# Gate projection of a branch merge made in two earlier stages and kept in DRAM

## What is computed

```python
h = rms_norm(x, g_mix_pre)
(lru_x, lru_gate, pool_in, q, k, v, q_idx, k_idx, w_idx,
 gate_logits) = split_columns(h @ w_in, IN_SIZES)
ya = rg_lru(conv(lru_x), ...) * gelu(lru_gate)        # recurrence
yb = multiscale_pool(pool_in, w_pool, pool_scale)
yc = dsa_attention(q, k, v, q_idx, k_idx, w_idx)      # index masks, attention
up = einsum('bsnc,ncd->bsnd', stack([ya, yb, yc], axis=2), w_branch)
gates = sigmoid(gate_logits.reshape(b, s, 3, 1024) + b_gate)
merged = sum(gates * up, axis=2)
```

## Time and profile before

| | us |
|---|---|
| median of 3 runs | 4222.14 (4216.18 to 4222.91) |
| the profiled execution, its own time | 4222.38 |
| its span, first to last instruction | 4220.3 |
| recurrence | 58.4 |
| index masks | 105.1 |
| attention and turn | 110.7 |
| merge | 225.4 |

### The profile page before, as it was taken

The page is one execution under the profiler, slowest core; times in us unless marked ns, Lnnn a source line. Parts: engine busy times, 40 slices in busy tenths (PEclk is TensorE's granted clock), DMA queues, the critical chain, the costliest instruction groups (busy, mean ns, idle before and its releaser), DMA issues. The chain is left out here.

```text
span 4220.3 us, 45269 instructions
## 1 busy us (share of the span) xinstructions
PE 3577.3 (85%) x17433; PEld 2585.9 (61%) x17433; DVE 2311.1 (55%) x2911; ACT 1676.4 (40%) x2523; POOL 1518.4 (36%) x748
## 2 busy tenths in 40 slices
PE   5999979967969999965996999995925999568997
PEld 3778869954446666652664555554813666447876
DVE  1047747662179999915656999991087211223310
ACT  2111223332047777630543777773122211343222
POOL 3323323540056666620013666652210122114442
PEclk8989989988969999987997999997855699789998
DMA  5324543332079999824007999991100023122230
GB/s 212 137 75 159 171 160 101 124 115 91 25 295 380 383 385 384 325 93 142 1 6 264 374 378 379 378 334 62 63 5 0 11 90 115 40 84 91 80 120 35
DMA packets 300593, 703.76 MB, mean 167 GB/s; under 512 B 15760, under 2 KB 62700, under 8 KB 297308
## 3 DMA queue, kind: packets, MB, share of 16 engines
q1 hardware_dynamic: 293552, 679.69, 43.5%
q0 software_dynamic: 6144, 20.98, 2.3%
q10 hardware_dynamic: 684, 0.21, 0.0%
HBM read 653.59 MB, written 47.25 MB: 166 GB/s over the span
## 5 line engine op out<-in xcount | busy, mean ns | idle before, releaser
L133 POOL TENSOR_TENSOR weights_low<-ring,weights_high 128x1024 fp32r<-128x1024 f32 (+2 forms) x210 | 494.2, 2359 | 1243.3 <-ACT weights_high L126 1235.8
L579 PE MATMUL ps<-h_parts,weights_high 128*128 128x512 f32 (+2 forms) x2528 | 738.9, 378 | 32.3 <-POOL weights_low L133 32.3
L579 PEld LDWEIGHTS ps<-h_parts,weights_high 128*128 128x128 f32 (+1 forms) x2528 | 461.9, 190 | 139.8 <-POOL weights_low L133 35.2
L579 PE MATMUL ps<-h_parts,weights_low 128*128 128x512 f32 (+2 forms) x1264 | 474.2, 375 | 0.0
L1723 DVE TENSOR_TENSOR more_low<-area,more_high 128x1024 fp32r<-128x1024 f32 x192 | 330.5, 1760 | 0.0
L1690 ACT ACTIVATE weights_high<-ring 128x1024 fp32r<-128x1024 f32 x256 | 271.1, 1061 | 136.0 <-PE ps L1623 91.8
L1690 ACT ACTIVATE more_high<-area 128x1024 fp32r<-128x1024 f32 x256 | 271.8, 1062 | 85.9 <-PE ps L1623 85.8
L1723 DVE TENSOR_TENSOR weights_low<-ring,weights_high 128x1024 fp32r<-128x1024 f32 x192 | 300.2, 1616 | 2.7 <-ACT weights_high L1690 2.7
L1594 POOL TENSOR_TENSOR more_low<-area,more_high 128x1024 fp32r<-128x1024 f32 x64 | 243.7, 3807 | 109.5 <-ACT more_high L1690 109.5
L126 ACT ACTIVATE weights_high<-ring 128x1024 fp32r<-128x1024 f32 (+1 forms) x158 | 161.8, 1040 | 279.8 <-PE ps L579 229.8
L579 PE MATMUL ps<-weights_high,h_parts 128*128 128x512 f32 (+2 forms) x832 | 253.3, 386 | 19.5 <-POOL weights_low L133 19.5
(11 more groups left out here) (427 smaller groups left out, 7532.4 us busy)
## 6 DMA issues: line engine op xcount, KB each, us to landing
ring<-in_moe_w SPq DMA_DIRECT2D x96, 2048.0 KB, 10.4
area<-in_moe_w SPq DMA_DIRECT2D x96, 2048.0 KB, 10.1
ring<-in_ada_w SPq DMA_DIRECT2D x24, 2048.0 KB, 8.3
ring<-in_ssd_in_w SPq DMA_DIRECT2D x12, 2048.0 KB, 10.9
ring<-in_w_in SPq DMA_DIRECT2D x11, 2048.0 KB, 7.6
ring<-in_w_ffn_in SPq DMA_DIRECT2D x10, 2048.0 KB, 7.9
area<-x_dram SPq DMA_DIRECT2D x18, 1024.0 KB, 5.0
ring<-in_ssd_out_w SPq DMA_DIRECT2D x4, 2048.0 KB, 7.9
```

The costliest lines, as they stand in the source:

```text
L133: pool.tensor_tensor(lo, views[k][:, ks, cols], hi, ALU.subtract).then_inc(self.low_p, 1)
L579: mm = pe.matmul(out, a, b, start=start and n == 0, stop=stop and n == 2)
```

## The change

The 24 gate tiles leave the merge. A class `Gates` makes them elsewhere: chunks 0 and 1 (8 tiles) in the recurrence, with one result buffer, chunks 2 to 5 (16 tiles) in the index masks, with two. A finished sigmoid is stored in DRAM (256 KB a tile), and the merge reads the gates back, 1 MB a chunk, into two buffers. In the ring's plan the six gate chunks now come first, then the six branch chunks. The PSUM banks 4 and 5 hold the gate tiles, and the pool products move to banks 0 to 3. The index masks' relus get four buffers in place of two. The merge uses all eight banks for branch tiles.

```diff
+class Gates:
+    def __init__(self, env, st, h, chunks, banks, bufs):
...
+        self.gs = st.sb("gates", [P, bufs, LAT])
...
+    def highs(self, act, units):
+        self.cut = self.env.ring_.cut_after(act, self.cuts, self.views, self.cut, self.m0 + units)
+
+    def low(self, pool, u):
+        ring = self.env.ring_
+        ring.highs += 1
+        pool.wait_ge(ring.high_s, ring.highs)
+        ring.cut_low(pool, self.cuts, self.views, u)
+
+    def products(self, pe, u):
+        ring = self.env.ring_
+        if u >= 2:
+            pe.wait_ge(self.ready, u - 1)
+        pe.wait_ge(ring.low_p, self.b0 + u + 1)
...
+        for k in range(KD):
+            mm = products(pe, self.env.ps[:, self.banks[u % 2], :], (hi[:, k, :], lo[:, k, :]), tuple(x[:, k, :] for x in self.h),
+                          k == 0, k == KD - 1)
+        mm.then_inc(ring.done, 1)
+
+    def sigmoid(self, act, u):
...
+        act.wait_ge(self.env.ring_.done, self.m0 + u + 1)
+        if u >= self.bufs:
+            act.wait_ge(self.stored[u % self.bufs], 16 * (u // self.bufs))
+        act.activation(self.gs[:, u % self.bufs, :], self.env.ps[:, self.banks[u % 2], :], ACT.Sigmoid,
...
+        self.highs(act, u + 1)
+
+    def store(self, sp):
+        ring = self.env.ring_
+        for u in range(self.n):
+            if u % 4 == 0:
+                ring.load_to(sp, self.first + u // 4 + SLOTS)
+            sp.wait_ge(self.ready, u + 1)
+            sp.dma_start(self.env.gate_dram[4 * self.chunks[u // 4] + u % 4, :, :], self.gs[:, u % self.bufs, :]) \
+                .then_inc(self.stored[u % self.bufs], 16)
+        ring.load_to(sp, len(ring.ends) + SLOTS)
+        for stored in self.stored:
+            sp.wait_ge(stored, 16 * self.n // self.bufs)
...
@@ recurrence @@
+        @block.gpsimd
+        def _(pool):
+            for u in range(gates.n):
+                gates.low(pool, u)
 
         @block.tensor
         def _(pe):
+            gates.products(pe, 0)
             pe.wait_ge(w_in, 64)
             for c in range(4):
+                if c == 2:
+                    gates.products(pe, 1)
+                    gates.products(pe, 2)
...
+            for u in range(3, gates.n):
+                gates.products(pe, u)
...
             act.activation(sp_[1], sp_[1], ACT.Exp).then_inc(ex, 1)
+            gates.highs(act, 0)
+            gates.sigmoid(act, 0)
             act.wait_ge(scl, 1)
...
+                for u in (1, 2) if pair[0] == 0 else range(3, gates.n):
+                    gates.sigmoid(act, u)
...
 # index_masks
+            for t, units in enumerate(((0, 2), (2, 3), (3, 7), (7, gates.n))):
+                logits(t)
+                for u in range(*units):
+                    gates.products(pe, u)
             pe.wait_ge(w_in, 16)
+            pe.wait_ge(relu, len(order))
             for g in range(4):
...
-            pool.wait_ge(counted, 1)
-            for g in (0, 1):
-                window(pool, g, sums).then_inc(ready, 1)
+            for u in range(gates.n):
+                gates.low(pool, u)
+                if u == 5:
+                    pool.wait_ge(counted, 1)
+                    for g in (0, 1):
+                        window(pool, g, sums).then_inc(ready, 1)
...
+                    if n >= 4:
+                        act.wait_ge(used, n - 3)
...
+            gates.highs(act, 0)
+            upto = (4, 8, 12, 20, 20, 24, 24, 28, 28, 28) + (32,) * (gates.n - 9)
+            relus(0, upto[0])
+            for u in range(gates.n):
+                gates.sigmoid(act, u)
+                relus(upto[u], upto[u + 1])
...
 # merge
             for c in range(6):
+                if c >= 2:
+                    sp.wait_ge(used, 4 * (c - 1))
+                sp.dma_start(gs[:, c % 2, :, :], env.gate_dram[4 * c:4 * c + 4, :, :].rearrange("f p t -> p f t")).then_inc(gates_in[c % 2], 16)
+                ring.load_to(sp, first + c + SLOTS)
...
+                    if c >= 2:
+                        pe.wait_ge(used, 4 * (c - 2) + f + 1)
+                    for k in range(4):
+                        mm = pe.matmul(ps[:, 4 * (c % 2) + f, :], w[:, k, tile(f)], branches[n][:, k, :], start=k == 0, stop=k == 3)
...
+                dve.wait_ge(gates_in[c % 2], 16 * (c // 2 + 1))
```

More of the change, by code:

```diff
@@ L2489, in recurrence @@
+def recurrence(env, base, lx, gate, yT, h, chunks):
     ps, ins = env.ps, env.ins
@@ L2708, in _, with merge @@
                 dve.tensor_scalar(mask[:, t, 0:keys], mask[:, t, 0:keys], -1e30, None, ALU.mult)
-def merge(env, base, h, branches, acc, merged):
+def merge(env, base, branches, acc, merged):
     ps, ring = env.ps, env.ring_
     with Stage(env, base) as st:
-        gs = st.sb("gates", [P, 4, LAT])
+        gs = st.sb("gates", [P, 2, 4, LAT])
         tmp = st.sb("gated", [P, 2, LAT])
[L2718 to L2721, removed]
+        used = st.sem("ups_used")
+        gates_in = [st.sem("even_gates_in"), st.sem("odd_gates_in")]
+        first, m0 = ring.take([4] * 6)
         block = st.block()
@@ L2730, in _ @@
             for c in range(6):
-                dg, n = c // 3, c % 3
+                n = c % 3
+                ring.wait(pe, first + c)
+                w = ring.view(first + c, 4, HALF)
                 for f in range(4):
[L2733 to L2739, removed]
-                    mm.then_inc(ring.done, 1)
[L2741 to L2754, removed]
-        def _(act):
-            n_ = ring.cut_after(act, cuts, views, 0, m0)
-            for c in range(6):
-                dg, n = c // 3, c % 3
-                for f in range(4):
-                    act.wait_ge(ring.done, m0 + 8 * c + f + 1)
-                    if c >= 1:
-                        act.wait_ge(used, 4 * (c - 1) + f + 1)
-                    act.activation(gs[:, f, :], ps[:, f, :], ACT.Sigmoid, bias=col(env, "b_gate_2", n * KD + dg * 4 + f)).then_inc(sig, 1)
-                    n_ = ring.cut_after(act, cuts, views, n_, m0 + 8 * c + f + 1)
+                    if c >= 2:
+                        pe.wait_ge(used, 4 * (c - 2) + f + 1)
+                    for k in range(4):
+                        mm = pe.matmul(ps[:, 4 * (c % 2) + f, :], w[:, k, tile(f)], branches[n][:, k, :], start=k == 0, stop=k == 3)
+                    mm.then_inc(ring.done, 1)
         @block.vector
@@ L2769, in _ @@
                 dg, n = c // 3, c % 3
+                dve.wait_ge(gates_in[c % 2], 16 * (c // 2 + 1))
                 for f in range(4):
-                    dve.wait_ge(ring.done, m0 + 8 * c + 4 + f + 1)
-                    dve.wait_ge(sig, 4 * c + f + 1)
+                    dve.wait_ge(ring.done, m0 + 4 * c + f + 1)
                     m = acc[:, f, :]
@@ L3041, in build @@
         project(env, at, jobs)
-        recurrence(env, place["yb"], part["lx"], part["gate"], part["ya"])
+        recurrence(env, place["yb"], part["lx"], part["gate"], part["ya"], hp, (0, 1))
         mask = carve(env, spent, [P, NL, LAT])
-        index_masks(env, place["yc"], part["qi"], part["ki"], part["wi"], mask, part["pool"], part["yb"])
+        index_masks(env, place["yc"], part["qi"], part["ki"], part["wi"], mask, part["pool"], part["yb"], part["gate"], hp,
+                    (2, 3, 4, 5))
         o = carve(env, spent + NL * LAT, [P, NL, LAT])
```

67 lines of the change are left out of this document (41 added, 26 removed).

## The result

| | before | after |
|---|---|---|
| median, us | 4222.52 of 4 runs (4216.18 to 4227.47) | 4127.24 of 4 runs (4119.64 to 4130.44) |
| profiled execution, its span | 4222.38, 4220.3 | 4130.44, 4128.7 |
| recurrence | 58.4 | 78.9 |
| index masks | 105.1 | 126.8 |
| attention and turn | 110.7 | 110.3 |

The ratio is 0.9773, 95% interval 0.9754 to 0.9791: 95 us less. The stages are cut as before the change. Between the two spans the merge gives 138.0 us, the two earlier stages take 20.5 and 21.7, attention gives 0.4, and what follows the merge takes 0.5.

A forecast was written before the change was run, and what follows sets the result against it. It took TensorE to bound the merge and VectorE the recurrence and index masks, leaving TensorE some 127 us free. Sum: 4222.4 - 136.8 + 21 + 20 = 4126.6, given as 4127, range 4102 to 4154.

The forecast's parts named there:

- The merge: Merge stage without gate tiles: products 83.4, cold start 2.2, VectorE tail 3.0, so 88.6 us, 136.8 less.
- The recurrence: Recurrence stage with 8 gate tiles: +21 us on 58.4, bounds +7 and +30.
- The index masks: Index masks stage with 16 gate tiles: +20 us on 105.1, bounds +12 and +38.
- the idle time of TensorE behind relu 4: Index masks: TensorE idles 6.6 us, as sigmoid 1 stands behind relu 4, which wants VectorE's first sum.
- Here TensorE becomes the bound: Index masks: TensorE's chain sets the length, 126 us; VectorE also comes out at 125.
- The bound of 4145: Total time if MAX8 rounds in the index masks wait for GpSimd too, losing about 18 us more.
- MAX8: Top-k rounds of the index masks: MAX8, 694 ns for 512 elements, taken as not waiting for GpSimd's low parts.
- Attention: Attention stage: could start at full clock; counted as 0, bounds -3 and 0.
- the port's cost: Recurrence and index masks: rival that GpSimd's low parts find gaps, stages gain 7 and 12 us, 4105; chance 0.13.
- More waiting: Both stages: rival that all VectorE work or engines' programs wait more, 4148, up to 4165; chance 0.20.
- cold clock: Both stages: rival that TensorE stays at 1.2 GHz, a tile costing 10.2 us, total 4240; chance 0.03.
- unhidden gates: Both stages: rival that tiles stand in series with VectorE's chain, 134.4 us come back, 4220; chance 0.04.

The follow-up runs named there:

- e1: Changed kernel with all 24 gate tiles made in a stage of their own ahead of the recurrence; 4227.93 us.
- e2: Changed kernel with GpSimd writing zeros (a memset, which reads nothing) in place of each low part; 4107.86 us.
- e3: Changed kernel with VectorE making the recurrence's first four low parts behind the softplus, GpSimd the other four; 4123.37 us.
- e4: Changed kernel with gate sigmoid 3 on ScalarE between the sigmoids of tiles 2 and 3 in the recurrence; 4127.19 us.

## Why the prediction was right

The time was predicted as 4127 and measured as 4127.24. That the two agree within 1 us is luck: the four runs spread over 10.8 us, and the span of the profiled one holds 4.1 us from ahead of the changed stages. The sum itself is not luck. It says 95.8 us less, the changed stages and what follows them give 95.7, and the terms hold one by one within 2 us:

- *The merge*, 88.6 predicted, 87.4 measured. Both parts of TensorE's time were a little too long: the products, taken as 83.4, take 82.6 at a granted clock of 1.00 throughout (e1), and the start at 0.50, taken as 2.2, costs 1.7 (84.3 against 82.6). The tail is 3.0, and the reads of gates were hidden as said.
- *The recurrence*, 79 and 78.9, and its inside fits: the softplus alternation 9.66 us for 9.6; the last square roots 54.5 us into the stage for 55; VectorE done after 73.7 for 74; tiles 5 to 7 from 3119.8 to 3138.3, 18.5 us for 18.8. e2 shows the cause (13.8 us less without reads), e3 the softplus, e4 the tail. One thing I had not seen: sigmoid 5 waits for a store. Of the 6.14 us that ScalarE is idle before it, most is tile 5, done by about 3127.1 (sigmoid 6 begins at 3132.74, right behind tile 6, which takes 5.6), so the store holds it up by some 1.9. That costs nothing, since TensorE makes tile 6 in the other bank meanwhile, and only tile 7 wants sigmoid 5's.
- *The index masks*, 125 to 126 and 126.8 (the steps sum to 126, that is +20.9, and stand in the sum as +20). The length and most marks are right: VectorE's sums start 4.8 us later into the stage (6), the clock is 0.93. Wrong is the idle time of TensorE behind relu 4: 3.4 us for 6.6. VectorE's sums came 1.2 us sooner than I had them, and TensorE's first two tiles, priced at full clock as 11.2, ran from 3147.55 to 3160.25, 12.7 us, with the clock at 0.50 up to 3150.2. TensorE's chain then ends 123.8 us into the stage, with ScalarE's last copy, and not 126. Wrong in part is thus the step "Here TensorE becomes the bound". VectorE, which I gave 125, ends last, 126.5 us into the stage, and with two thirds of the gate matmuls gone the stage keeps 123.4. The two were nearly tied, so the sum didn't suffer; but whoever had taken TensorE's work for the thing to cut would have gained 3 us.
- *MAX8*, taken as not waiting: 695 ns, and MATCH_REPLACE8 676 over 512 elements. The bound of 4145 by its waiting is out.
- *Attention*, 0 predicted, 0.4 less.

The rivals: without the port's cost the stages would be 65.1 and 115.7 (e2); the rival had 65.4 and 117.1, and its total of 4105 stands beside e2's 4107.86. It was priced right, within 2 us a stage, and did not happen. More waiting, cold clock and unhidden gates are excluded by 78.9 and 126.8 us, the clocks of 0.86 and 0.93, and e1, which is the unhidden case at 4227.93 for the 4220 that I gave it.

## What to carry to other kernels

Work moved beside another engine's stage is worth its own time less what that stage's chain grows: here 138 us less 42. The growth can come from what the moved work does on a third engine. Here about 25 of the 42 us came with GpSimd's low parts, and the other 17 stand in e2 as well, and no run takes them apart. A long GpSimd instruction that reads cost most beside a chain of tiny VectorE ones: six steps of 1.35 us in all took 9.66 beside four low parts. And where two engines hand work to each other through one queue, find out which chain ends last and what in it is waiting. Here cutting the work of either engine alone gave 3 us or nothing, and changing the order between them gave 6.

## What the runs showed of the chip

- A two-input operation on VectorE waited for GpSimd's reads and not for its writes; TENSOR_SCALAR and COPY waited for writes too (0.96 and 1.04 us in e2). MAX8 and MATCH_REPLACE8 did not wait for a low part, which reads and writes: begun inside a low part (GpSimd from 3224.20 to 3226.61, MATCH_REPLACE8 at 3225.62 and MAX8 at 3226.23, of 384 elements) they take 0.54 and 0.56 us, like those outside. And a low part begun inside a RECIPROCAL (3120.75, in one from 3117.77 to 3121.12) takes its ordinary 2.37.
- A 256 KB store issued at 3122.90 in the recurrence, 2.8 us behind a 2 MB load on SyncE's queue, landed 6.0 us later, where the median of the stores is 2.2; sigmoid 5 began at 3129.02. The store before it, issued just ahead of that load, landed in time to start sigmoid 4 at 3122.19. That the load is the cause is likely and not tested.
- The same program ahead of the recurrence took from 3055.5 to 3064.6 us in the traces, 9 us apart; every single edit here but e2, which changes both stages, is worth less than that.
- Attention, which before the change had a granted clock of 0.50 from its start, now has 0.76 over its first 2 us (3268.8 to 3270.8) and then 0.50 to the end. TensorE was busy in 113 of the 126.8 us ahead of it, and idle for the last 3.7.
